# A decoder layer kernel: where one weight cast stands, the forget weights as one operand, and a block in two transfers

## What is computed

```python
h = rms_norm(x, norm_mix_g)                       # 256 x 1024
proj = einsum('bsd,dc->bsc', h, w_in)             # w_in 1024 x 3080
fq, fk, fv, f_logit, mq, mk, mv = split(proj, ...)  # 512,512,512,8,512,512,512 columns
log_f = log_sigmoid(f_logit + b_forget)           # per token and head
fox  = forgetting_attention(fq, fk, fv, log_f)
moba = moba_attention(rotary(mq), rotary(mk), mv)
x = x + concat(rms_norm(fox), rms_norm(moba)) @ w_out
x = x + hierarchical_moe(rms_norm(x), ...)        # 32 experts, w_gate/w_up/w_down 96 MB
return rms_norm(x)
```

## Time and profile before

| | |
|---|---|
| time, three runs | median 355.81 us (355.76 to 357.69) |
| the profiled execution | 356.66 us, its span 354.8 us |
| TensorE busy | 314.8 us, 89% of the span |
| VectorE, ScalarE, GpSimd busy | 167.0, 121.1, 46.2 us |
| moved by the DMA engines | 121.07 MB, mean 341 GB/s |
| mean granted TensorE clock | 0.976 |

### The profile page before, as it was taken

One profiled execution on the slowest core, in us unless ns is written; L12 is line 12 of the kernel. 1 busy time (PEld: TensorE's weight loads), 2 busy tenths in 40 slices (PEclk: granted clock), 3 DMA queues, 4 the chain that ended last, 5 costly groups with the idle time before them and its releaser, 6 DMA issues.

```text
span 354.8 us, 11527 instructions
## 1 busy us (share of the span) xinstructions
PE 314.8 (89%) x4766; PEld 244.4 (69%) x4767; DVE 167.0 (47%) x461; ACT 121.1 (34%) x308; POOL 46.2 (13%) x79
## 2 busy tenths in 40 slices
PE   8999999999999999979799899999999758649482
PEld 5999899799775446666577677777777555526460
DVE  4759285554164513844355355555555514322233
ACT  3544254463244237423233133333333302121113
POOL 3400001642504037600000000000000000000001
PEclk9999999999999999999999999999999989998878
DMA  7999994081849998699999999999999999999933
GB/s 270 321 388 386 386 396 171 14 342 21 336 136 388 307 400 328 235 294 411 421 404 385 413 421 409 417 421 414 422 417 414 413 413 426 414 416 420 415 127 118
DMA packets 33669, 121.07 MB, mean 341 GB/s; under 512 B 5624, under 2 KB 8080, under 8 KB 26480
## 3 DMA queue, kind: packets, MB, share of 16 engines
q1 hardware_dynamic: 33312, 120.63, 87.0%
q10 hardware_dynamic: 336, 0.14, 0.1%
HBM read 119.72 MB, written 1.05 MB: 340 GB/s over the span
## 4 chain that ended last, share of the span: by engine, by line
PE 69%; SPq 15%; DMA 6%; issue 3%; ACT 3%; DVE 2%; POOLq 0%; POOL 0%; ACTq 0%; DVEq 0%
PE bank L547 13%; PE bank L807 13%; SPq L389 8%; PE bank L614 7%; PE bank L839 6%; DMA spare<-in_w_up_dram 6%; PE bank L761 6%; PE bank L541 5%; SPq L401 5%; PE bank L768 3%; SPq L383 2%; PE bank L561 2%; PE bank L576 1%; PE bank L828 1%; PE bank L523 1%
## 5 line engine op out<-in xcount | busy, mean ns | idle before, releaser
L807 PE MATMUL bank<-ring,hT 128*32 128x128 f32 x1664 | 54.1, 283 | 18.7 <-DMA ring<-in_w_up_dram 8.7
L807 PEld LDWEIGHTS bank<-ring,hT 128*32 128x32 f32 x1664 | 47.7, 114 | 27.6 <-issue 27.4
L1546 DVE SCALAR_TENSOR_TENSOR yb<-bank,pp,yb 64x512 fp32r<-64x512 f32 x34 | 25.5, 750 | 50.8 <-ACT yb L1080 50.3
L1263 DVE TENSOR_TENSOR unit_lo<-ring,unit_hi 128x2048 fp32r<-128x2048 f32 (+1 forms) x12 | 26.5, 2209 | 28.7 <-ACT unit_hi L909 28.7
L1080 ACT ACTIVATE yb<-bank,pp 64x512 fp32r<-64x512 f32 x34 | 23.2, 683 | 35.4 <-PE bank L839 35.0
L761 PEld LDWEIGHTS bank<-pp,qk 128*128 128x128 bf16 x912 | 29.1, 100 | 8.1 <-issue 5.6
L761 PE MATMUL bank<-pp,qk 128*128 128x64 bf16 x912 | 31.4, 196 | 2.8 <-issue 2.8
L614 PE MATMUL bank<-ring,qk 128*128 128x512 f32 (+1 forms) x72 | 29.9, 551 | 0.0
L1225 POOL TENSOR_SCALAR stats<-qk 128x1 f32<-128x1 f32 x2 | 0.6, 311 | 200.5 <-ACT work L1100 200.5
L807 PE MATMUL bank<-work,hT 128*32 128x128 f32 x320 | 21.4, 288 | 5.4 <-DMA spare<-in_w_up_dram 2.9
L1529 DVE SCALAR_TENSOR_TENSOR pp<-bank,stats,pp 128x128 f32<-128x128 f32 x18 | 6.3, 351 | 41.5 <-ACT pp L1069 41.5
(11 more groups left out here) (217 smaller groups left out, 527.4 us busy)
## 6 DMA issues: line engine op xcount, KB each, us to landing
ring<-in_w_up_dram SPq DMA_DIRECT2D x24, 1024.0 KB, 16.7
ring<-in_w_down_dram SPq DMA_DIRECT2D x24, 1024.0 KB, 17.4
ring<-in_w_gate_dram SPq DMA_DIRECT2D x16, 1024.0 KB, 15.9
ring<-in_w_in_dram SPq DMA_DIRECT2D x5, 2048.0 KB, 19.7
ring<-in_w_gate_dram SPq DMA_DIRECT2D x16, 512.0 KB, 13.8
ring<-in_w_out_dram SPq DMA_DIRECT2D x4, 1024.0 KB, 12.8
spare<-in_w_gate_dram SPq DMA_DIRECT2D x4, 1024.0 KB, 18.7
spare<-in_w_up_dram SPq DMA_DIRECT2D x4, 1024.0 KB, 19.1
```

The source lines that it names most:

```text
L807: last = mm(p_gu[b:b + CAP, w * P:(w + 1) * P], hg[:, k, CAP * e:CAP * (e + 1)], w_gu[at[e]][:, w, k, h, :], start=(k == 0), stop=(k == KD ...
L1263: V.tensor_tensor(unit_lo[b][:, k, :], unit_src(u)[:, k, :], unit_hi[b][:, k, :].bitcast(fp32), ALU.subtract).then_inc(w_lo_ready, 1)
L1546: V.scalar_tensor_tensor(out=yb[half][rest, :], in0=p_y[rows, :], scalar=wcol[rows, :], in1=yb[half][rows, :].bitcast(fp32), op0=ALU.mult, ...
```

## The change

Four edits, all in the first 40 us:

1. ScalarE's cast of the second half of unit 0's weights stands between the fourth and the fifth copy of `h_hi`; it stood behind the eighth.
2. `wf_hi` and `wf_lo` lie in one operand `wf_both` of 40 columns: 0 to 7 the high part, 32 to 39 the low part, 8 to 31 zeros that GpSimd writes at the start. TensorE multiplies it with `h_hi` and with `h_lo`: 2 times 8 steps into 40 rows. VectorE takes rows 0 to 7 and rows 32 to 39, each scaled, and adds them. (The product of the low part and `h_lo` is computed now too.)
3. Block 1 is loaded in two transfers of 1 MB (units 2 and 3) with a semaphore each. `wf` and the bias `b_forget` are issued between the two, so behind unit 2.
4. The other small tables are issued behind unit 3, ahead of block 2.

```diff
-        wf_hi, wf_lo = part("wf_hi", ring_at + 4 * (T0 + 2528), N_FOX), part("wf_lo", ring_at + 4 * (T0 + 2592), N_FOX)
+        WF_W = 32 + N_FOX
+        wf_both = part("wf_both", ring_at + 4 * (T0 + 2528), WF_W)
+        wf_hi, wf_lo = wf_both[:, :, 0:N_FOX], wf_both[:, :, 32:WF_W]
...
-                    sp.dma_start(wf, I["w_in"][0, :, 3 * FOX_W:3 * FOX_W + N_FOX].rearrange("(k p) c -> p k c", p=P)).then_inc(wf_in, 16)
+                elif b == 1:
+                    for u in (2, 3):
+                        c = c0 + (u - 2) * UNIT
+                        sp.dma_start(unit_src(u), I["w_in"][0, :, c:c + UNIT].rearrange("(k p) c -> p k c", p=P)).then_inc(unit_in[u], 16)
+                        if u == 2:
+                            sp.dma_start(wf, I["w_in"][0, :, 3 * FOX_W:3 * FOX_W + N_FOX].rearrange("(k p) c -> p k c", p=P)).then_inc(wf_in, 16)
+                            sp.dma_start(bfg, I["b_forget"][0].rearrange("(h o) -> h o", o=1)).then_inc(bfg_in, 16)
                 else:
-                    if b == 1:
+                    if b == 2:
                         sp.dma_start(cb[:, :], I["const_bf16"]).then_inc(fg_in, 16)
                         sp.dma_start(neg8, I["const_neg8"]).then_inc(fg_in, 16)
-                        sp.dma_start(bfg, I["b_forget"][0].rearrange("(h o) -> h o", o=1)).then_inc(fg_in, 16)
...
             pe.wait_ge(wf_lo_ready, 1)
-            for n, (w, h) in enumerate(((wf_hi, h_hi), (wf_hi, h_lo), (wf_lo, h_hi))):
+            pe.wait_ge(wf_pad, 1)
+            for n, h in enumerate((h_hi, h_lo)):
                 for k in range(KD):
-                    last = mm(bank[O_BANK][0:N_FOX, 0:SEQ], w[:, k, :], h[:, k, :], start=(n == 0 and k == 0), stop=(n == 2 and k == KD - 1))
+                    last = mm(bank[O_BANK][0:WF_W, 0:SEQ], wf_both[:, k, :], h[:, k, :], start=(n == 0 and k == 0), stop=(n == 1 and k == KD - 1))
...
             for k in range(KD):
                 act.wait_ge(tr_done, k // 2 + 1)
+                if k == KD // 2:
+                    act.wait_ge(unit_in[0], 16)
+                    nc.scalar.copy(unit_hi[0][:, k:KD, :], unit_src(0)[:, k:KD, :]).then_inc(w_hi_ready, 1)
                 A(h_hi[:, k, :], bank[4 + k // 2][:, (k % 2) * SEQ:(k % 2 + 1) * SEQ], ACT.Copy, scale=gcol[:, k:k + 1]).then_inc(h_hi_ready, 1)
-            k = slice(KD // 2, KD)
-            act.wait_ge(unit_in[0], 16)
-            nc.scalar.copy(unit_hi[0][:, k, :], unit_src(0)[:, k, :]).then_inc(w_hi_ready, 1)
...
+            nc.gpsimd.memset(wf_both[:, :, N_FOX:32].bitcast(fp32), 0.0).then_inc(wf_pad, 1)
...
-            step(V.tensor_tensor(fz, bank[O_BANK][0:N_FOX, 0:SEQ], rootrow[0:N_FOX, :], ALU.mult))
-            dve.wait_ge(fg_in, 48)
+            for n, dst in enumerate((fz, fc)):
+                rows = slice(32 * n, 32 * n + N_FOX)
+                last = V.tensor_tensor(dst, bank[O_BANK][rows, 0:SEQ], rootrow[rows, :], ALU.mult)
+            step(last)
+            step(V.tensor_tensor(fz, fz, fc, ALU.add))
+            dve.wait_ge(bfg_in, 16)
```

More of the change, by code:

```diff
@@ L274, in layer_program @@
         fg_in, gmoe_in, bias_in, gfin_in = (sem(n) for n in ("fg_in", "gmoe_in", "bias_in", "gfin_in"))
-        unit_in = [sem(f"unit_in{u}") for u in range(2)]
+        unit_in = [sem(f"unit_in{u}") for u in range(4)]
+        bfg_in, wf_pad = sem("bfg_in"), sem("wf_pad")
         first_in = sem("first_in")
@@ L640, in _ @@
             pe.wait_ge(fc_ready, 1)
-            pe.wait_ge(fg_in, 48)
+            pe.wait_ge(fg_in, 32)
             scores(0)
@@ L895, in wait_unit_in @@
             def wait_unit_in(u):
-                if u < 2:
+                if u < 4:
                     act.wait_ge(unit_in[u], 16)
```

## The result

The changed kernel took 354.9 us (median of 20 runs), the kernel before 357.43 us in 20 runs beside it; the ratio is 0.9948, its 95% interval 0.9925 to 0.9972. That is 1.9 us less, with 1.0 to 2.7 us as the bounds. (The two medians are 2.5 us apart; the ratio is made from the fast runs alone and is not their quotient.) The forecast had 1.20 us less, so 0.9966, inside the interval. Two things show at once: the median of the kernel before is 1.6 us higher over these 20 runs than over the three of them that are shown ahead, and single runs of one kernel spread over 5 to 6 us, several times the effect. So the runs tell that it is faster, and the traces have to tell by how much and where.

A forecast was written before the change was run, and what follows sets the result against it. TensorE was taken to bound the kernel up to about 150 us, the expert-weight stream behind that. Gains of 0.30 (cast), 0.90 (forget product) and 0 (transfers) sum to 1.20: 355.81 - 1.20 = 354.6 us, range 353.6 to 356.2.

The forecast's parts named there:

- slower feed: Unit 0's second half: copies come each 0.36 us and pace TensorE, so the 0.63 us stall yields only 0.30.
- rival D: Unit 0: ScalarE's copies keep ahead of TensorE, giving the whole 0.63 and 0.93, 354.2 us; chance 0.10.
- The most is the whole stall, 0.63: Upper bound for moving the cast: TensorE's 0.63 us wait ahead of unit 0's second half.
- ScalarE idle for about 0.4 us ahead of L936: Sign that the forecast is right: ScalarE waits about 0.4 us for the second half's data before its cast.
- The wider load: Forget product: the 40-column weight load runs beside the matmul before it; estimated 27 ns more for 32 more columns.
- the limit of 20.5 us: Forget weights may land up to 20.5 us without cost; forecast landing about 15.5 to 17.5.
- block 2 was to land 0.9 us later: Block 1 in 1 KB rows takes 6.0 instead of 5.1 us, delaying block 2 by 0.9 us, at no cost.
- Carrying over: From projection to loop: the 1.20 us gained by 40 us is kept; the weight stream starts and ends that much sooner.
- rival A: Loop: the weight stream takes up the gain, leaving 355.8 us; chance 0.12.
- can't be what sets the start of the stream: Between projection and loop: the weight queue has run empty at 141 us, so the stream starts 1.20 us sooner.
- Every issue behind it too: Sign that the forecast is right: all issues after the first `w_out` issue also come 1.2 us earlier.
- Rival B: SyncE's in-order issue: forget weights land at 22.1 us, TensorE waits 1.6, loss 0.4, 356.2 us; chance 0.08.

The follow-up runs named there:

- after: First profiled execution of the changed kernel, nothing further changed; its span was 353.1 us.
- e5_wflate: Changed kernel with the forget weights' transfer issued behind unit 3 instead of ahead of it; span 356.0 us.
- e5b_wflater: Changed kernel with the forget weights' transfer issued behind block 2; span 362.2 us.
- the dose of 5.6 us: Changed kernel with the 16 forget matmuls done four times over, 48 more matmuls; ratio to the kernel before 1.0184.
- the first pair: First profiled executions of the kernel before and the changed kernel, spans 354.8 and 353.1 us; the second pair repeats both, 353.7 and 351.0.
- e7_dvecast: Changed kernel with the cast of unit 0's second half on VectorE, ahead of the fifth h_lo, instead of ScalarE; ratio to the kernel before 0.9982.
- e9_poolwait: e7_dvecast with GpSimd's low part of the first half held back until VectorE's cast of the second half is through; span 356.4 us.
- e3_transfers: Kernel before with only the transfer changes: block 1 in two transfers, forget weights behind unit 2, tables behind unit 3; ratio 0.9993.

## Why the prediction was right, point by point

- **Edit 1**, forecast 0.30 us. The mechanism was right to the details: gap gone, half of it back as a slower feed; second half forecast at 10.78, found 10.85; low parts 13.08 and 13.16, the low part of VectorE just in time. The size was too large for the pair it was read from (0.22 at the start of unit 1) and too small for a mean. The failing term is the assumption that the profiled execution stood for all: its first copy was the earliest of the four with the cast last (7.34 of 7.34 to 7.94), so its stall was the smallest. On a mean it is 0.4 to 0.5 us, between the forecast and rival D's 0.63; rival D's reason was wrong, since the copies do not keep ahead.
- Two readings in it were off and changed nothing. "The most is the whole stall, 0.63" counts from the modelled end of the last matmul; by starts, eight matmuls cost 0.96, so TensorE could have gone on at 9.61 + 0.96 = 10.57, 0.79 us ahead of 11.36. And TensorE would ask for unit 1's low part at 17.66 - 0.30 = 17.36, not 17.24; it asked at 17.44, with the part ready at 16.48 (14.19 + 2.29).
- "ScalarE idle for about 0.4 us ahead of L936" did not show in after: the copies started 0.36 later in that execution and ended as the data landed. It is the same assumption; with earlier copies the idle time is there, 0.44 us in e5_wflate (first copy at 7.30) and 0.60 in e5b_wflater (7.08).
- **Edit 2**, forecast 0.90: 0.88 (2.79 less 1.91). The wider load cost 0.003 us a matmul (1.91/16 against 2.79/24).
- **Edits 3 and 4**, forecast 0: 0. The forget weights were cast at 15.86, within the 15.5 to 17.5 forecast, and the limit of 20.5 us was crossed only where e5b_wflater put them. One term of it failed, without effect on the sum: block 2 was to land 0.9 us later because block 1 now comes in shorter rows, and unit 4's cast started at 26.80, against 26.85 before. The shorter rows were slower, as forecast (349 GB/s from 16 to 18 us, 409 before). The small tables held the engines at 245 GB/s from 12 to 15 us before and at 231 from 18 to 21 now. What gave the 0.9 us back, no run separates.
- **Carrying over** (rival A): up to 150 us each shift arrived whole, in fourteen executions. Behind it the stream does not absorb the dose of 5.6 us, and has a spread of 3.7 us of its own. That a queue run empty "can't be what sets the start of the stream" was right; that the last landing would come 1.2 us sooner could not be read from one pair (0.50 in the first, 2.66 in the second). "Every issue behind it too" was not quite so: the first `w_out` issue came 1.10 us earlier (35.16 against 36.26), but the two issues of expert weights near 42 and 45 us came 0.48 and 0.40 later, behind `w_out` issues that took 7.66 us instead of 6.08; from the next one on (68.17 against 69.27) nearly all came about 1.1 us earlier.
- **Rival B** fell in e5_wflate. The reason against it, that the old 9.5 us was mostly standing behind others, held: the landing time was 9.8 us with unit 2 ahead.
- **The sum**: the first score came 1.10 us earlier in the first pair and 1.24 in the second. With edit 1 on a mean the front gained 0.41 or 0.49, plus 0.88, so 1.3 to 1.4 us; the runs say 1.9 with 1.0 to 2.7. The forecast's 1.20 lies in it, and so does the front's gain. Whether the half microsecond between the front and the runs is more than noise, nothing here shows.
- **The time itself** was hit with some luck: 354.6 us forecast, 354.9 measured. The forecast subtracted 1.20 from a median of three runs, 355.81; over 20 runs the median of the kernel before is 357.43, and 1.20 less than that is 356.2.

## What to carry to other kernels

A stall ahead of an engine has a size only for one execution; look at what its two ends hang on. Here one end hung on a chain that wandered by up to 0.9 us, and the edit tied it to a landing that hardly moves, which on a mean was worth more than the 0.22 us that one pair of profiles showed. And where single runs spread by several times the effect, read an edit at a landmark a short way behind it, and show once, by a dose that is large against the spread, that landmarks carry to the end.

## What the runs showed of the hardware that was not expected

- **An issue can take 3 us, whatever its own size.** `b_forget` is 32 bytes. Its issue took 0.37 us in the kernel before and 3.00 in the changed one, where unit 2 and the forget weights are issued right ahead of it; the 1 MB of unit 3 behind it took 0.38. It looks as if the issue waits for room in the queue: the two long ones here end at 9.11 and 12.15, just ahead of the casts of the second half of unit 0 (9.28) and of unit 1 (12.24), which wait for their data. That is a reading; no run varied what stands in the queue for its sake. SyncE's timeline in the changed kernel (start us, us):

```profile
6.03 3.08 SPq L373 DMA_DIRECT2D ring<-in_w_in_dram  x1
...
9.15 3.00 SPq L374 DMA_DIRECT2D ring<-in_b_forget_dram  x1
...
12.19 0.38 SPq L371 DMA_DIRECT2D ring<-in_w_in_dram  x1
```

- **A wait of TensorE can cost more than its length**: in e5b_wflater 6.3 us of waiting, then some 5 us of work at the clock of 1.2 GHz, 2.4 us lost on top. It need not: the wait of 2.28 us in the first turns of the loop was followed by the full clock in after. In the last couple of experts the clock is worth up to 1.7 us from one execution to another (1.95 to 3.64 us for 64 matmuls).
- **A VectorE cast can take double beside GpSimd**: 1.46 against 0.68 us (e7_dvecast, e9_poolwait).
- **Shorter rows load slower**: from 16 to 18 us the DMA engines moved 409 GB/s in the kernel before, in rows of 2 KB, and 349 in the changed one and 356 in e3_transfers, in rows of 1 KB; their busy share was 1.05 to 1.13 in all three.
- **The entry of the loop** can cost TensorE 3.37 us for nothing that the trace records, against 0.31 to 0.34 in all the other executions. Why stays open.
